# Attention in memory of its own, and the last layer's three branches merged in another order

## What is computed

```python
def hybrid_layer_2(...):
    px = split_cols(hx @ w_in + b_in)
    pc = split_cols(hc @ w_in + b_in)
    ya_x = conv_module(*px[0:3], dw_w, dw_b, ln_g, ln_b, w_conv_out)
    yb_x, yb_c = gla_branch(px[3:9], pc[3:9], ...)
    yc_x, yc_c = attn_branch(px[9:13], pc[9:13], ...)
    def merge(p, ya, yb, yc):
        return (jax.nn.sigmoid(p[13]) * ya + jax.nn.sigmoid(p[14]) * yb
                + jax.nn.sigmoid(p[15]) * yc) @ w_out
    xs = xs + gate_x[:, None] * merge(px, ya_x, yb_x, yc_x)
    if need_ctx:
        ...
```

## Time and profile before

| what | us |
|---|---|
| median of 3 runs | 1394.38 (1392.98 to 1394.94) |
| the profiled execution, its own time | 1394.86 |
| its span in the profile | 1393.5 |
| TensorE busy | 1314.5 |
| VectorE busy | 870.2 |
| ScalarE busy | 584.5 |
| GpSimd busy | 281.6 |

### The profile page before, as it was taken

How to read it: one execution, slowest core, us unless ns; L and a number is a source line. 1 busy time by engine, 2 the same in 40 slices (tenths; PEclk the granted TensorE clock), 3 DMA queues, 4 the chain that set the end, 5 groups by cost and what they waited for, 6 DMA issues and landing times.

```text
span 1393.5 us, 18891 instructions
## 1 busy us (share of the span) xinstructions
PE 1314.5 (94%) x7490; PEld 1037.0 (74%) x7490; DVE 870.2 (62%) x1496; ACT 584.5 (42%) x967; POOL 281.6 (20%) x217
## 2 busy tenths in 40 slices
PE   7999987999979999997999999999999998799998
PEld 5777766777757777775777887777898876488876
DVE  4795756685677542499996522424576688845553
ACT  3444533344454445222434532323463663356442
POOL 0110013100033322247000011311252142201112
PEclk9999998999999999999999999999999999989999
DMA  7674465363433411121111222223553333123451
GB/s 250 226 269 143 143 242 190 129 226 136 164 109 109 152 51 61 46 75 61 62 46 46 64 88 91 91 91 93 165 166 99 103 106 105 47 85 118 145 176 66
DMA packets 49192, 168.46 MB, mean 121 GB/s; under 512 B 5862, under 2 KB 7078, under 8 KB 48848
## 3 DMA queue, kind: packets, MB, share of 16 engines
q1 hardware_dynamic: 49104, 167.26, 36.0%
HBM read 166.19 MB, written 1.05 MB: 120 GB/s over the span
## 4 chain that ended last, share of the span: by engine, by line
PE 74%; DVE 10%; issue 10%; POOL 4%; ACT 1%; DMA 1%; SPq 0%; POOLq 0%; DVEq 0%; ACTq 0%
PE bank L1493 16%; PE bank L1494 15%; PE bank L1495 15%; PE bank L1412 3%; PE bank L1806 3%; DVE conv_val L2555 3%; PE bank L1511 3%; PE bank L1512 2%; PE bank L1513 2%; DVE w_lo L2235 2%; PE bank L1573 2%; PE bank L1781 1%; PE bank L1536 1%; PE bank L1426 1%; PE bank L1742 1%
## 5 line engine op out<-in xcount | busy, mean ns | idle before, releaser
L1493 PE MATMUL bank<-w_hi,x_hi 128*128 128x512 f32 (+4 forms) x1120 | 466.4, 416 | 18.1 <-DVE x_lo L2245 12.3
L2235 DVE TENSOR_TENSOR w_lo<-w_raw,w_hi 128x1024 fp32r<-128x1024 f32 (+3 forms) x264 | 322.4, 1224 | 252.3 <-ACT w_hi L1843 252.2
L1843 ACT ACTIVATE w_hi<-w_raw 128x1024 fp32r<-128x1024 f32 (+3 forms) x264 | 269.8, 1026 | 442.6 <-PE bank L1495 249.9
L1494 PE MATMUL bank<-w_lo,x_hi 128*128 128x512 f32 (+4 forms) x1120 | 436.4, 390 | 0.0
L1495 PE MATMUL bank<-w_hi,x_lo 128*128 128x512 f32 (+4 forms) x1120 | 435.7, 389 | 0.0
L1493 PEld LDWEIGHTS bank<-w_hi,x_hi 128*128 128x128 f32 x1120 | 215.8, 193 | 72.0 <-DVE x_lo L2245 15.5
L1495 PEld LDWEIGHTS bank<-w_hi,x_lo 128*128 128x128 f32 x1120 | 214.0, 191 | 46.4
L1494 PEld LDWEIGHTS bank<-w_lo,x_hi 128*128 128x128 f32 x1120 | 215.3, 192 | 38.7
L2555 DVE SCALAR_TENSOR_TENSOR conv_val<-conv_u,par,conv_val 128x512 f32<-128x512 f32 (+1 forms) x240 | 150.2, 674 | 0.0
L2875 POOL TENSOR_TENSOR merged<-merged,sigma 128x512 f32<-128x512 f32 x24 | 37.4, 1585 | 178.6 <-DVE sigma L2597 178.6
L1511 PE MATMUL bank<-x_hi,w_hi 128*128 128x512 f32 (+1 forms) x192 | 67.0, 349 | 0.5 <-ACT conv_val L2045 0.5
(11 more groups left out here) (330 smaller groups left out, 1727.2 us busy)
## 6 DMA issues: line engine op xcount, KB each, us to landing
w_raw<-in_w SPq DMA_DIRECT2D x172, 512.0 KB, 3.5
w_raw<-in_wm SPq DMA_DIRECT2D x48, 512.0 KB, 5.1
w_raw<-in_wo SPq DMA_DIRECT2D x40, 512.0 KB, 3.5
w_raw<-in_wy_gla SPq DMA_DIRECT2D x8, 512.0 KB, 3.5
w_raw<-in_wy_att SPq DMA_DIRECT2D x8, 512.0 KB, 3.5
w_raw<-in_wy_conv SPq DMA_DIRECT2D x8, 512.0 KB, 3.5
w_raw<-in_w SPq DMA_DIRECT2D x8, 460.0 KB, 5.5
w_raw<-in_w SPq DMA_DIRECT2D x12, 288.0 KB, 2.8
```

Of the source, the lines that this page charges most:

```text
L1493: mm(out, xh[:, q, col], hi[:, kk, 0:w], start=kp == 0 and kk == 0 and not with_bias, stop=False)
L1494: mm(out, xh[:, q, col], lo[:, kk, 0:w], start=False, stop=False)
L1843: do(hi, raw, ACT.Copy).then_inc(sem["cut_hi"], 1)
L2235: v.tensor_tensor(lo, raw, hi.bitcast(F32), ALU.subtract).then_inc(sem["cut_lo"], 1)
```

## The change

Attention gets memory of its own, so that its keys and queries, scores and maxima no longer wait for the end of linear attention. The transposed queries are written over the queries (`b.aq`), the keys' tile, the statistics and one of three probability buffers lie in new places, and two probability buffers and the two transposed ones lie in the last layer where `x_hi`, `x_lo` of the context tokens were (free once the last projection of the context, chunk `GV`, is done). In layer 0 two probability buffers and the transposed ones stay where they were, so there the keys and queries move ahead, but scores are still planned behind the end of linear attention, and `a_exp` waits for it. The last layer merges linear attention, attention, convolution (1, 2, 0) instead of (1, 0, 2).

```diff
-BRANCHES = [(1, 2, 0), (1, 0, 2)]
+BRANCHES = [(1, 2, 0), (1, 2, 0)]
...
-    "ak_flip": lambda l: normed(l, "k") + [("gla_o", l, 1), ("gla_st", l, 0, 3, 1)],
+    "ak_flip": lambda l: normed(l, "k"),
...
-    "aq_flip": lambda l, j: normed(l, "q") + [("gla_o", l, 1)],
+    "aq_flip": lambda l, j: normed(l, "q"),
...
-    "a_s": lambda l, qt, j: [("aq_act", l, 2), ("aq_dve", l, 3), ("ak_t", l)],
+    "a_s": lambda l, qt, j: [("aq_act", l, 2), ("aq_dve", l, 3), ("ak_t", l)] + over_attention(l),
...
+def over_attention(l):
+
+    return [("gla_o", l, 1), ("gla_st", l, 0, 3, 1)] if l < LAYERS - 1 else [("project", "in2", l, GV, NP - 1, 3)]
...
+        with ExitStack() as scope:
+            b.lent = [sb(n, [P, KD, 2 * S], F32, scope) for n in ("lent_prob", "lent_turned")]
...
-            b.aq_t, b.ak_t = sb("att_q_t", [P, AH // 2, 512], F32, scope), sb("att_k_t", [P, 512], F32, scope)
-            b.aprob, b.astat = sb("att_p", [P, 3, 512], F32, scope), sb("att_stat", [P, 2, 24], F32, scope)
+            sb("beside", [P, 5, 512], F32, scope)
+            b.aprob = sb("att_p", [P, 2, 512], F32, scope)
...
+        sb("under", [P, 9, 512])
+        b.ak_t, b.aprob_2, b.astat = sb("att_k_t", [P, 512]), sb("att_p_2", [P, 512]), sb("att_stat", [P, 2, 24])
...
+    def prob_home(self, l, qt, j):
+
+        b, p = self.b, self.slot("a_prob", l, qt, j)[0]
+        if p == 2:
+            return b.aprob_2.rearrange("p (a b) -> p a b", a=2)
+        if l == LAYERS - 1:
+            return b.lent[0][:, 4 + 2 * p:6 + 2 * p, S:2 * S]
+        return b.aprob[:, p].rearrange("p (a b) -> p a b", a=2)
...
-        act.wait_ge("gla_o", l, 1)
         act.wait_ge("aq_flip", l, j)
-        do(b.aq_t[:, j, 0:n], ps[:, 0:n], ACT.Copy, scale=HD ** -0.5).then_inc(sem["aq_act"], 1)
+        do(b.aq[:, 0:n // P, j * P:(j + 1) * P], ps[:, 0:n].rearrange("p (t q) -> p t q", q=P), ACT.Copy, scale=HD ** -0.5).then_inc(sem["aq_act"], 1)
...
         act.wait_ge("a_max", l, qt, j)
+        if l < LAYERS - 1:
+            act.wait_ge("gla_o", l, 1)
+            act.wait_ge("gla_st", l, 0, 3, 1)
+        else:
+            act.wait_ge("project", "in2", l, GV, NP - 1, 3)
```

More of the change, by code:

```diff
@@ L946, in before_flip, with over_operand @@
     earlier = branch_before(l, i)
-    return [("gla_o", l, 1) if earlier is None else ("project", f"y{earlier}", l, 1, 1, tiles_of(l)[-1])]
+    if earlier is None:
+        return over_operand(l)
+    return [("project", f"y{earlier}", l, 1, 1, tiles_of(l)[-1])]
+def over_operand(l):
+    return [("gla_o", l, 1)] if l < LAYERS - 1 else [("project", "in2", l, GV, NP - 1, 3)]
+def over_attention(l):
+    return [("gla_o", l, 1), ("gla_st", l, 0, 3, 1)] if l < LAYERS - 1 else [("project", "in2", l, GV, NP - 1, 3)]
 def normed(l, what):
@@ L1781, in a_s @@
                 ins = mm(k.bank[slot("aux", "a_s", l, qt, j)[0]][:, g * keys:(g + 1) * keys],
-                         b.aq_t[rows, h % 4, qt * P:(qt + 1) * P], b.ak_t[rows, k0:k0 + keys], start=True, stop=True)
+                         b.aq[rows, qt, h % 4 * P:(h % 4 + 1) * P], b.ak_t[rows, k0:k0 + keys], start=True, stop=True)
         ins.then_inc(sem["a_s"], 1)
@@ L1786, in a_flip @@
         i, before = slot("aux", "a_flip", l, qt, j)
-        prob = b.aprob[:, slot("a_prob", l, qt, j)[0]]
+        prob = k.prob_home(l, qt, j)
         pe.wait_ge("a_exp", l, qt, j)
         pe.wait_ge(*(before or ()))
-        flips(k.bank[i], [prob[:, c * P:(c + 1) * P] for c in range(4)]).then_inc(sem["a_flip"], 1)
+        flips(k.bank[i], [prob[:, c // 2, c % 2 * P:(c % 2 + 1) * P] for c in range(4)]).then_inc(sem["a_flip"], 1)
     def a_v(l, qt, j):
         i, before = slot("sum2", l, qt)
-        turned = b.aprob_t[:, slot("a_prob_t", l, qt, j)[0]]
+        turned = k.turned_home(l, qt, j)
         key_tiles = EVERY if qt in X_TILES else C_TILES
@@ L1805, in a_v @@
             for c, t in enumerate(key_tiles):
-                ins = mm(k.bank[i][:, at * HD:(at + 1) * HD], turned[:, (g * nb + c) * P:(g * nb + c + 1) * P],
+                ins = mm(k.bank[i][:, at * HD:(at + 1) * HD], turned[:, (g * nb + c) // 2, (g * nb + c) % 2 * P:((g * nb + c) % 2 + 1) * P],
                          b.kkv[:, t, QK2 + P + kh * HD:QK2 + P + (kh + 1) * HD], start=c == 0, stop=c == nb - 1)
@@ L1871, in flip_hi @@
             earlier = branch_before(l, int(source[1]))
-            act.wait_ge(*(("gla_o", l, 1) if earlier is None else ("project", f"y{earlier}", l, 1, 1, tiles_of(l)[-1])))
+            act.wait_ge(*over_operand(l)[0] if earlier is None else ("project", f"y{earlier}", l, 1, 1, tiles_of(l)[-1]))
         elif source == "merged":
@@ L2181, in a_exp @@
             h = places(qt, j)[g]
-            ins = do(b.aprob[:, p, g * keys:(g + 1) * keys], ps[:, g * keys:(g + 1) * keys], ACT.Exp,
+            ins = do(prob[:, g * halves:(g + 1) * halves, :],
+                     ps[:, g * keys:(g + 1) * keys].rearrange("p (a b) -> p a b", a=halves), ACT.Exp,
                      bias=stat[:, h:h + 1], accum_out=stat[:, AH + h:AH + h + 1])
@@ L2711, in ak_t @@
         ps = k.bank[slot("aux", "ak_flip", l)[0]]
-        dve.wait_ge("gla_o", l, 1)
-        dve.wait_ge("gla_st", l, 0, 3, 1)
         dve.wait_ge("ak_flip", l)
@@ L2719, in aq_dve @@
         ps = k.bank[slot("aux", "aq_flip", l, j)[0]]
-        dve.wait_ge("gla_o", l, 1)
         dve.wait_ge("aq_flip", l, j)
-        v.tensor_scalar(b.aq_t[:, j, 0:n], ps[:, 0:n], HD ** -0.5, None, ALU.mult).then_inc(sem["aq_dve"], 1)
+        v.tensor_scalar(b.aq[:, 0:n // P, j * P:(j + 1) * P], ps[:, 0:n].rearrange("p (t q) -> p t q", q=P), HD ** -0.5, None,
+                        ALU.mult).then_inc(sem["aq_dve"], 1)
     def a_max(l, qt, j):
```

10 lines of the change are left out of this document (8 added, 2 removed).

## The result

| | us |
|---|---|
| changed kernel, median of 4 runs | 1405.65 (1403.15 to 1406.28) |
| kernel before, beside it, median of 4 runs | 1394.4 |
| ratio, with its 95% interval | 1.0079 (1.0067 to 1.0090) |
| span of the profiled execution, before and after | 1393.5 and 1404.1 |

The kernel became slower by 11.3 us. The forecast was 1399.9 us, its range ended at 1405.0. The sign was right; the size was half of what came.

What follows compares the result with a forecast made beforehand. TensorE, busy 1314.5 of 1393.5 us, was taken as the bound, so only its idle time and low clock could change. -4.0 + 9.0 + 0.5 = +5.5 us gave 1399.9 us, range 1390.0 to 1405.0.

Steps and rivals of the forecast that it cites:

- A: Last layer, from the last projection ahead of `gla_o` to the merge gate's second chunk: 10.3 us against 14.3, -4.0 us.
- C: TensorE's 4.46 us stall for `gla_la` at 1155.13 us: less work fits ahead of it, +0.5 us.
- B: Attention's last heads and `y2` of the second query tile, no projection between: 6.2 us idle, 3.0 low clock, +9.0 us.
- A, idle time: TensorE's waits around attention's start in the last layer: 8.3 us idle in the new order, against 8.7 before.
- the walk: Step-by-step working of the new order around attention's start, with lengths from profile rows, giving each wait of TensorE.
- A, low clock: Around attention's start the clock falls once more, for less work: between none and 3.15 us, taken as 2.0.
- rival 3: Slower still: clock low as long as A's earlier 13.6 us; 3 us more in B, 2 in A; 1404.9 us, chance 0.15.
- That adds nothing: they are TensorE's own work, in another place: Moving key and query transposes and two pairs of scores ahead among projections was costed at no added work.
- The cover of the convolution's branch: The last branch's chain from gate to low part, some 5 us, is covered by eight half projections, 11.3 us.
- The edits costed at nothing: Exponentials and copies write the same 512 columns elsewhere, at most in two runs of 256: no cost.
- The table load: ScalarE's load ahead of A's second pair of exponentials: counted at 1.28 us; by the skill page 1.4 us more.
- Rival 2: Faster: A fills, idling some 2.5 us at full clock, and B keeps its clock; 1389.1 us, chance 0.2.

Runs made afterwards that it cites:

- apart_only: The changed kernel with the last layer's branches put back to (1, 0, 2), attention keeping its own memory: 1397.61 us, 1.0025 of the kernel before.
- pairs_split: The kernel before, planner putting off the second step of a `gla_con` or `gla_a` pair by 0.9 us in the last layer: 1398.76 us against 1394.31.
- pairs_after: The changed kernel with only a planner rule keeping pairs of `gla_con` and `gla_a` together in the last layer: 1399.83 us, 1.0041 of the kernel before.
- pairs_fill_a: `apart_only` with `gla_con` and `gla_a` pairs kept together and linear attention's second gate chunk ahead of `y1`: 1376.57 us, 0.9868 of the kernel before.

## Why the prediction was wrong in size

Its sum was -4.0 + 9.0 + 0.5 = +5.5 us; the medians say +11.3, the profiled spans +10.6. By the account the 5.1 us between +5.5 and +10.6 are, to 0.1 us: A 3.1 more than forecast, work 3.2, the fall ahead of the last layer 1.4, C 0.1, less 1.6 in B and 1.0 at the end.

- **A, idle time: right.** "8.3 us idle, against 8.7"; it was 7.9, and the waits are those of the walk: 0.8 for "0.85", 0.5 and 0.7 for "1.35", 1.9 for "1.1", 0.8 for "0.7", 1.8 for "2.3", 1.5 for "1.7", all with the releasers named. One row was read wrongly on the way: the three taps called alone (1.27 us, at 1198.60) have GpSimd beside them too, on four columns; those of 2.05 us stand beside its work on 512:

```profile
1198.77 1.18 POOL L2922 TENSOR_TENSOR gla_ms<-gla_ms,minus_half 128x4 f32<-128x4 f32 x1 [1.56 <-DVE gla_ms L2665]
```

- **A, low clock: the first step that failed.** "Between none and 3.15 I take 2.0." The low clock cost 5.4 us, as it had before (5.5), for 13.5 us. The row it was sized by was a stretch of 6.3 us in C; the row of A itself, 13.6 us, was at hand and was left for rival 3. In every run with 7 us or more of waits there without more cover it cost 4.0 to 7.8. So A gained 0.9 us and not 4.0: 3.4 too little by the clock, 0.4 of it made good by the idle time. What held the clock low for that long was not tried beyond that it goes with the waits.
- **"That adds nothing: they are TensorE's own work, in another place": the second step that failed.** With the scores ahead, half projections came to stand between the two steps of more pairs that share the array. The changed kernel has 3.2 us more work, and by kind 2.0 of it are those steps, with three runs more of them (`apart_only`: 2.1 more work, 1.9 of it by kind). `pairs_split` priced seven at 5.2 us, and `pairs_after` took 5.8 us off the changed kernel, part of that by projections left over for A. Nothing in the rows shown of before gave it away, but the groups of 16 and of 8 matmuls with one length were in the timeline.
- **B: right.** "+9.0" (6.0 idle and 3.0 of low clock); 8.0 by the medians of the changed kernel and `apart_only`; by the account 5.2 idle, 2.2 low clock and 1.1 of work. The longest wait was `gated` of `att_q`, as named, 2.19 us. Two slips stand in its working: the waits that it names (0.85, 1.1, 0.3 and 3.7) add up to 5.95 and not 6.2, and "3.4 us at most" charges the low clock to idle time too. With the 7.16 us that TensorE was busy, the same rows give 2.2, which is what B showed.
- **C: right by its size, partly by luck.** "+0.5": -1.0 idle and +1.6 of low clock, and a second execution of the kernel before shows 1.4 us of that by itself.
- **The cover of the convolution's branch: right**, 0.28 us idle in 63.4. The edits costed at nothing on ScalarE and VectorE show as 0.5 us less and 1.8 us more busy time on the whole.
- **The table load.** "It is 1.28 us in the trace, and I count that." In the changed kernel it stands right behind the copy and right ahead of the exponential:

```profile
1205.96 0.60 ACT L2228 ACTIVATE lent_turned<-bank 128x512 f32<-128x512 f32 x1 [0.74 <-PE bank L1443]
1206.57 1.28 ACT L2218 ACT_TABLE_LOAD   x1
1207.87 0.69 ACT L2218 ACTIVATE att_p<-bank,att_stat 128x512 f32<-128x512 f32 x1
```

From the copy's end (1206.56) to the exponential are 1.31 us. The Trainium skill, "ScalarE: Activation LUTs", "What ACT_TABLE_LOAD costs", gives 2.66 us with a drain; no drain shows here, and the measurement decides: the 1.4 us more that the prediction worked out by the page did not come.

Rival 3 of the prediction (slower still, 1404.9 us) came within 0.8 us of the median, and that by luck. It had the length of the low clock in A right, but put 2 us more on it where 3.4 came, gave B 6.0 us of low clock where 2.2 came, and had no term for the work. Rival 2's 1389.1 us lay outside the range that was said to hold most of it.

## What to carry to other kernels

A stall of TensorE is cured by work that needs nothing, kept back for it, and not by moving its waits apart: A stayed as it was under a change made of memory, fell to 2.9 us idle with 11.3 us of projections put ahead of what they do not depend on, and was gone when four half projections more were left for it (`pairs_fill_a`). When steps are moved into a sequence, look at which others come to stand apart: two steps on opposite halves of the array that stood together ran at the price of one (0.78 us against 0.77), and each pair put apart cost 0.74 us. And price the clock by the place itself: in all nine profiles here with 7 us or more of waits in A, the cluster that had lowered it before lowered it again.
